# Gated attention scores computed as narrow blocks instead of whole 128 by 128 squares

## What is computed

```
cum = cumsum(log_g); decay[i,j,d] = exp(cum[i,d] - cum[j,d]) for j <= i, else 0
scores[i,j] = sum_d q[i,d] k[j,d] decay[i,j,d]
o = scores @ v + (q * exp(cum)) @ state
state = exp(last) * state + (k * exp(last - cum))^T v
```

## Time and profile before

| | |
|---|---|
| median of 3 runs | 2903.11 us |
| the profiled execution's own time | 2903.8 us |
| its span (first to last instruction) | 2902.0 us |
| PE busy | 98% of the span |
| DVE, ACT, POOL busy | 63%, 39%, 47% |
| the gated stage's levels | 1424.9 to 1939.4 us, 48 levels in 6 jobs |

### The profile page before, as it was taken

The page is one execution under the profiler, slowest core; times in us unless marked ns, Lnnn a source line. Parts: engine busy times, 40 slices in busy tenths (PEclk is TensorE's granted clock), DMA queues, the critical chain, the costliest instruction groups (busy, mean ns, idle before and its releaser), DMA issues.

```text
span 2902.0 us, 36401 instructions
## 1 busy us (share of the span) xinstructions
PE 2852.6 (98%) x14022; PEld 2353.8 (81%) x14022; DVE 1824.9 (63%) x2853; ACT 1133.9 (39%) x1649; POOL 1372.6 (47%) x693
## 2 busy tenths in 40 slices
PE   8999999999999999999999999999999999999998
PEld 7777787888888877777888888888888788888886
DVE  8847776555568766555647755642463766647786
ACT  4323354444443334343434544523231644433331
POOL 4435348977758652111211211112122699857774
PEclk9999999999999999999999999999999999999999
DMA  6342202332355322112101111124322144463441
GB/s 220 88 127 77 96 28 87 102 106 95 113 181 182 103 78 85 51 52 72 45 30 52 51 59 59 44 73 160 137 98 92 66 143 148 160 221 120 159 145 73
DMA packets 114300, 295.79 MB, mean 102 GB/s; under 512 B 14544, under 2 KB 23168, under 8 KB 114112
## 3 DMA queue, kind: packets, MB, share of 16 engines
q1 hardware_dynamic: 114128, 293.46, 30.3%
HBM read 216.61 MB, written 76.81 MB: 101 GB/s over the span
## 4 chain that ended last, share of the span: by engine, by line
PE 87%; DVE 7%; ACT 2%; issue 2%; POOL 2%; DMA 0%; SPq 0%; ACTq 0%; DVEq 0%; POOLq 0%
PE PS L509 29%; PE PS L951 21%; PE PS L1110 4%; PE PS L1109 4%; PE PS L1108 4%; PE PS L1364 3%; PE PS L558 2%; PE PS L559 2%; PE PS L560 2%; PE PS L1232 1%; PE PS L1262 1%; PE PS L1130 1%; PE PS L1128 1%; PE PS L1129 1%; PE PS L847 1%
## 5 line engine op out<-in xcount | busy, mean ns | idle before, releaser
L3205 POOL TENSOR_TENSOR WL<-WR,WH 128x1024 fp32r<-128x1024 f32 x236 | 584.0, 2479 | 1163.4 <-ACT WH L1482 1163.3
L1482 ACT ACTIVATE WH<-WR 128x1024 fp32r<-128x1024 f32 x237 | 248.7, 1054 | 285.0 <-POOL WR L3245 144.2
L509 PE MATMUL PS<-XH,WH 128*128 128x512 f32 x1040 | 338.5, 407 | 9.0 <-DVE XL L2260 9.0
L509 PE MATMUL PS<-XL,WH 128*128 128x512 f32 x1040 | 322.8, 392 | 0.0
L509 PE MATMUL PS<-XH,WL 128*128 128x512 f32 x1040 | 321.7, 390 | 0.0
L951 PE MATMUL PS<-XH,WH 128*128 128x512 f32 x624 | 243.5, 390 | 6.0 <-DVE XL L2574 5.0
L951 PE MATMUL PS<-XH,WL 128*128 128x512 f32 x624 | 242.8, 389 | 0.0
L951 PE MATMUL PS<-XL,WH 128*128 128x512 f32 x624 | 242.8, 389 | 0.0
L2789 DVE TENSOR_TENSOR XF<-XF,PS 128x512 f32<-128x512 f32 x280 | 186.1, 682 | 72.9 <-PE PS L1110 72.6
L509 PEld LDWEIGHTS PS<-XH,WL 128*128 128x128 f32 x1040 | 195.5, 188 | 42.8
L509 PEld LDWEIGHTS PS<-XL,WH 128*128 128x128 f32 x1040 | 195.8, 188 | 42.5
(11 more groups left out here) (408 smaller groups left out, 6102.7 us busy)
## 6 DMA issues: line engine op xcount, KB each, us to landing
WR<-in_weights SPq DMA_DIRECT2D x201, 512.0 KB, 3.6
HR<-hsum SPq DMA_DIRECT2D x70, 512.0 KB, 3.6
hsum<-CT SPq DMA_DIRECT2D x40, 512.0 KB, 3.1
DW<-in_weights SPq DMA_DIRECT2D x40, 512.0 KB, 6.7
hsum<-CT SPq DMA_DIRECT2D x40, 256.0 KB, 2.4
gates<-EG SPq DMA_DIRECT2D x18, 512.0 KB, 5.2
EI<-gates SPq DMA_DIRECT2D x18, 512.0 KB, 5.2
hbuf<-CT SPq DMA_DIRECT2D x14, 512.0 KB, 3.3
```

What stands on the lines that cost most here:

```text
L509: last = e.matmul(PS[:, u.b + h, :], w, x[:, k, 512 * h:512 * h + 512], start=k == 0 and w is w1 and x is xh, stop=k == nk - 1 and w is w2)
L1482: e.activation(WH[:, v % NSPL, :], raw_at(r), ACT.Copy).then_inc(w_hi, 1)
L3205: e.tensor_tensor(WL[:, v % NSPL, :], raw_at(r), WH[:, v % NSPL, :].bitcast(F), ALU.subtract).then_inc(w_lo, 1)
```

## The change

TensorE: levels 0, 1 and 2 are computed by level_blocks, as the exact blocks: one block of 64 keys by 64 queries a chunk, two of 32 by 32, four of 16 by 16. Levels 3 to 6 and the diagonal are computed by square_blocks: four blocks of 32 keys a chunk, each by 16 queries (the second halves of the spans within those 32 columns, a strided operand), or by all 32 queries for the diagonal. A block's output lies at its keys' partitions (0, 32, 64 or 96), so one level takes one bank for each head instead of two.

VectorE: levels 0 to 2 are plain copies, one, two and four for each head (keep_blocks); levels 3 to 7 are four masked copies of 32 partitions for each head. All wait for the level's last matmul. The output matmuls wait for nh copies of level 7 instead of 2 nh. Scaling, exponentials, ticks and everything else are as before.

```diff
+BLOCKS = ((0,), (0, 64), (0, 32, 64, 96))
+        def second_halves(x, n):
+            z = LEVELS[n]
+            if len(x.shape) == 3:
+                return x.rearrange("p i (m c) -> p i m c", c=2 * z)[:, :, :, z:2 * z]
+            return x.rearrange("p (m c) -> p m c", c=2 * z)[:, :, z:2 * z]
...
+                def square_blocks(n):
+                    us = [claim(e, ("lv", j, n, 1, hh)) for hh in range(nh)]
+                    kl, kr = (KQ[:, n % 2, :],) * 2 if n < 7 else (K_, Q_)
+                    if n < 7:
+                        e.wait_ge(c_kq, 7 * j + n + 1)
+                    for i in range(8):
+                        for hh in range(nh):
+                            for b in range(0, 128, 32):
+                                c = 128 * i + b
+                                o, x = PS[b:b + 32, us[hh].b, 32 * i:32 * i + 32], kr[rows[hh], c:c + 32]
+                                if n < 7:
+                                    o, x = second_halves(o, n), second_halves(x, n)
+                                last = e.matmul(o, kl[rows[hh], c:c + 32], x, start=True, stop=True)
+                            if i == 7:
+                                last.then_inc(us[hh].full, 1)
+                def level_blocks(n):
+                    s, us = LEVELS[n], [claim(e, ("lv", j, n, 1, hh)) for hh in range(nh)]
+                    e.wait_ge(c_kq, 7 * j + n + 1)
+                    for i in range(8):
+                        for hh in range(nh):
+                            for b in BLOCKS[n]:
+                                c = 128 * i + b
+                                last = e.matmul(PS[b:b + s, us[hh].b, s * i:s * i + s], KQ[rows[hh], n % 2, c:c + s],
+                                                KQ[rows[hh], n % 2, c + s:c + 2 * s], start=True, stop=True)
+                            if i == 7:
+                                last.then_inc(us[hh].full, 1)
...
-                    us = [[claim(e, ("lv", j, n, g, hh)) for hh in range(nh)] for g in range(2)]
-                    if n < 7:
-                        e.wait_ge(c_kq, 7 * j + n + 1)
-                    for g in range(2):
-                        for i in range(4 * g, 4 * g + 4):
-                            for hh in range(nh):
-                                c = slice(128 * i, 128 * i + 128)
-                                last = e.matmul(PS[:, us[g][hh].b, 128 * (i % 4):128 * (i % 4) + 128], kl[rows[hh], c],
-                                                kr[rows[hh], c], start=True, stop=True)
-                                if i % 4 == 3:
-                                    last.then_inc(us[g][hh].full, 1)
+                    if n < len(BLOCKS):
+                        level_blocks(n)
+                        tick(fill, per[1][n])
+                        continue
+                    square_blocks(n)
...
+            def keep_blocks(j, n):
+                s = LEVELS[n]
+                for hh in range(gated_job(j)[0]):
+                    u = lots["lv", j, n, 1, hh]
...
+                    e.wait_ge(u.full, u.nfull)
+                    for b in BLOCKS[n]:
+                        o = ST[b:b + s, hh, :].rearrange("p (i c) -> p i c", c=128)[:, :, b + s:b + 2 * s]
+                        t = e.tensor_copy(o, PS[b:b + s, u.b, 0:8 * s].rearrange("p (i c) -> p i c", c=s))
+                        t.then_inc(u.drained, 1) if b == BLOCKS[n][-1] else t.then_inc(dve, cv.up())
...
-                        e.copy_predicated(o, LV[:, n:n + 1, :].to_broadcast([128, 4, 128]), four(u)).then_inc(u.drained, 1)
+                    for b in range(0, 128, 32):
+                        r = slice(b, b + 32)
+                        o = ST[r, hh, :].rearrange("p (i c) -> p i c", c=128)[:, :, r]
+                        x = PS[r, u.b, 0:256].rearrange("p (i c) -> p i c", c=32)
+                        m = LV[r, n:n + 1, r]
+                        if n < 7:
+                            k = 16 // LEVELS[n]
+                            o, x = second_halves(o, n), second_halves(x, n)
+                            m = second_halves(m, n).to_broadcast([32, 8, k, LEVELS[n]])
+                        else:
+                            m = m.to_broadcast([32, 8, 32])
+                        t = e.copy_predicated(o, m, x)
+                        t.then_inc(u.drained, 1) if b == 96 else t.then_inc(dve, cv.up())
```

More of the change, by code:

```diff
@@ L1352, in compute @@
                 tick(fill, per[0])
                 for n in range(8):
-                    kl = kr = KQ[:, n % 2, :]
-                    if n == 7:
-                        kl, kr = K_[:, :], Q_[:, :]
-                    us = [[claim(e, ("lv", j, n, g, hh)) for hh in range(nh)] for g in range(2)]
-                    if n < 7:
-                        e.wait_ge(c_kq, 7 * j + n + 1)
-                    for g in range(2):
-                        for i in range(4 * g, 4 * g + 4):
-                            for hh in range(nh):
-                                c = slice(128 * i, 128 * i + 128)
-                                last = e.matmul(PS[:, us[g][hh].b, 128 * (i % 4):128 * (i % 4) + 128], kl[rows[hh], c],
-                                                kr[rows[hh], c], start=True, stop=True)
-                                if i % 4 == 3:
-                                    last.then_inc(us[g][hh].full, 1)
+                    if n < len(BLOCKS):
+                        level_blocks(n)
+                        tick(fill, per[1][n])
+                        continue
@@ L1388, in compute @@
                         e.wait_ge(c_sg, j + 2)
[L1389 to L1392, removed]
+                        for hh in range(nh):
+                            k = lots["lv", j, 7, 1, hh]
+                            e.wait_ge(k.drained, k.ndrained)
                     else:
@@ L2999, in gates @@
                     yield
+            def keep_blocks(j, n):
+                s = LEVELS[n]
+                for hh in range(gated_job(j)[0]):
+                    u = lots["lv", j, n, 1, hh]
+                    if n == 0:
+                        e.wait_ge(c_st, j + 1)
+                    else:
+                        p = lots["lv", j, n - 1, 1, hh]
+                        e.wait_ge(p.drained, p.ndrained)
+                    e.wait_ge(u.full, u.nfull)
[3 more added lines that the diff above has]
+                        t.then_inc(u.drained, 1) if b == BLOCKS[n][-1] else t.then_inc(dve, cv.up())
@@ L3001, in keep @@
             def keep(j, n):
                 nh = gated_job(j)[0]
[L3003 to L3008, removed]
-                        else:
-                            p = lots["lv", j, n - 1, g, hh]
-                            e.wait_ge(p.drained, p.ndrained)
-                        e.wait_ge(u.full, u.nfull)
-                        e.copy_predicated(o, LV[:, n:n + 1, :].to_broadcast([128, 4, 128]), four(u)).then_inc(u.drained, 1)
+                if n < len(BLOCKS):
+                    keep_blocks(j, n)
+                    return
@@ new lines, in keep @@
+                for hh in range(nh):
+                    u, p = lots["lv", j, n, 1, hh], lots["lv", j, n - 1, 1, hh]
+                    e.wait_ge(p.drained, p.ndrained)
+                    e.wait_ge(u.full, u.nfull)
+                    for b in range(0, 128, 32):
[7 more added lines that the diff above has]
+                            m = second_halves(m, n).to_broadcast([32, 8, k, LEVELS[n]])
+                        else:
+                            m = m.to_broadcast([32, 8, 32])
+                        t = e.copy_predicated(o, m, x)
+                        t.then_inc(u.drained, 1) if b == 96 else t.then_inc(dve, cv.up())
```

## The result

The changed kernel takes 2877.41 us (median of 4 runs, 2873.02 to 2877.69) against 2903.33 for the kernel before: ratio 0.9902, 95% interval 0.989 to 0.9914, 25.9 us less. 2874.7 was forecast. The profiled execution took 2877.36 us with a span of 2875.6.

What follows compares the result with a forecast made beforehand. TensorE, busy 98% of the span, was taken as the bound. Levels -28.2 us, bank waits -1.6 and new KQ waits +1.4 made -28.4 on 2903.8, or 2875.4; the median, 0.7 lower, 2874.7 us, range 2862 to 2921.

Steps and rivals of the forecast that it cites:

- A level before: TensorE's levels in the old kernel: net 1.79 us each with one head, 2.19 with two, 92.5 us in all.
- Changing the tile: TensorE, every level after the change: leaving the 128 by 128 tile costs 0.45 us, 48 levels 21.6 us.
- One tile by itself: TensorE, one tile's records: 0.057 us each at 64 columns, 0.032 at 32; level 0 takes 0.91 us a head.
- The starting rate: TensorE's levels: records on different tiles start 11 ns apart, so 64 take 0.70 us and 128 take 1.41.
- Side by side: TensorE: four groups of 32 output columns were taken to overlap as two groups of 64 do in the trace.
- VectorE's copies: VectorE after the levels: 128-column copies cost about 0.22 us, saving 22 us over 8 heads, worth nothing in itself.
- What is late next: TensorE reaches KQ sooner: level 2 waits about 0.46 us in jobs 2, 3 and 4, 1.4 us in all.
- It just holds: KQ before level 5, 1.66 us early: levels 1 to 4 shrink by 2.75 us, the chain's copies by 1.2, so no wait.
- a slow starting rate: Rivals on TensorE's issue in four-block levels: 24 ns a record gives 2916 us (chance 0.14), 54 ns gives 3018 (0.04).
- blocks in turn: Rival in TensorE's levels: 32-column groups take turns, 31 ns a record, only the two heads overlap; 2913 us, chance 0.06.

Runs made afterwards that it cites:

- same_tile_run: The changed kernel with loops turned round in levels 3 to 7, so all eight chunks of one 32-key block stand in a row; 2897.3 us.
- steps_moved: The changed kernel with filling steps of jobs 1 to 4 moved from the last levels to before the levels that wait; 2865.2 us.

## Why the prediction was right, and where it was not

The direction, the place and nearly the size (-28.4 forecast, -25.9 measured) were right, and so was the mechanism on TensorE. That the sum came within 2.5 us is partly luck: TensorE's own gain was put 14 us too low, and 13 us of losses were put too low or not seen (6.6 of waits for KQ, 2.3 more in the levels, 4.1 outside them), besides 3.1 us lost before the stage.

- *A level before*: 2.19 and 1.79 us, exact but for the diagonals (2.25 and 1.90).
- *Changing the tile*, 0.45 us: measured about 0.31 (0.87 less 64 x 8.8 ns), so 48 levels paid 15, not 21.6.
- *One tile by itself*: level 0 was put at 0.91 + 0.45 = 1.36 and took 1.28; level 1 at 0.96 and took 0.83.
- *The starting rate*, the unknown: 11 ns taken, 8.1 to 9.0 measured, over up to 128 records in a row. The floor of about 25 ns that the Trainium skill gives, "TensorE: Matmul & The Clock Gate", section "Wait — 56ns, not 53.3ns?", does not hold across tiles here, and the measurement decides; within one tile 27.2 ns was seen, which the load explains. Together these made 42 us of undisturbed gain instead of 28.
- *Side by side*: four groups of 32 columns do run together, if their matmuls alternate; same_tile_run shows that the loop order carries 20 us of the gain.
- *VectorE's copies*, 0.22 each: the term that failed. VectorE was to save 22 us and saved none. It took the slope of wide copies and their overlap; the narrow ones cost 0.32, 0.46 for the finest levels. The upper bound of 0.35 was nearer.
- *What is late next*: level 2 was forecast to wait 0.46 us and waited 0.57. "It just holds" for level 5 was wrong, 0.4 us before level 4 and 1.1 before level 5 in three jobs, 1.9 in job 1: TensorE saved more than forecast and VectorE less. 8.0 us, of which I had 1.4.
- *Not foreseen at all*: stalls for instructions (1.7 us by the rows) and the slow stretch in job 1 (up to 3.4 us).
- *The rivals*: a slow starting rate (24 or 54 ns a record) and blocks in turn (31 ns) are refuted by 8.5 ns.

## What to carry to other kernels

Small float32 blocks pay on TensorE when consecutive matmuls go to different tiles. Two bounds then have to be worked out, and the larger counts: the records of a level times 8 to 9 ns, and the records on one tile times the time of one there, 27 ns on 32 columns and 58 to 62 ns on 64. With 32-column tiles in turn the columns streamed, 16 or 32, hardly mattered. Cutting a copy into pieces by partitions doesn't make it cheaper on VectorE, and where TensorE's saving eats the slack of a chain that runs beside it, move filler work to the place of the wait, which here was worth as much as half the change. Weigh the number of instructions too: two blocks of 64 beat four of 32 where two heads already fill the rows, and lost to them with one head.

## What was unexpected

- TensorE stalls, of up to 2.5 us, always behind the 193rd instruction of a block of 256, once a level has 128 records (256 instructions in 1.1 us). With 64 records a level none inside a level was seen. Each ends 1.2 to 1.5 us after a packet of 256 instructions has landed. Why the packet comes no sooner stays open.
- The granted clock falls to 1.2 GHz for single stretches in places that differ between executions and kernels (345, 428, 1377, 2250 us among them) in code that never changed; each costs up to 1.7 us, and together they blur differences under 3 us. What brings them stays open: behind the same gap of 2.5 us at about 424 us the kernel before ran on at 2.4 GHz and steps_moved at 1.2 GHz for 3.4 us, and the stretch at 1379.6 us of the changed kernel followed 13 us in which TensorE was never idle.
